# Second block's borders: the queries' projection k-tile by k-tile with the meta tokens turned later, squares of H beside its additions, lambda's exponentials behind the keys' conversions

## The reference, cut to what matters

```
h = concatenate([meta, x])                       # x: the first block's rms_norm(h, final_norm)
for l in range(2):
    hn = rmsnorm(h, norm_gain[l])
    proj = hn @ w_in[l]                          # dq dk dv dg fq fk fv ff fg
    dq, dk = partial_rope(dq), partial_rope(dk)
    lam = exp(sum(lambda_q1*lambda_k1)) - exp(sum(lambda_q2*lambda_k2)) + lam_init
    do = rmsnorm(diff_attention(dq, dk, dv, lam)) * (1 - lam_init) * silu(dg)
    fo = forgetting_attention(fq, fk, fv, cumsum(log_sigmoid(ff + bias))) * silu(fg)
    h = h + concatenate([do, fo]) @ w_out[l]
out = rmsnorm(h, final_gain)                     # the 256 rows behind the meta tokens
```

## Time and profile before

| | us |
|---|---|
| median of 3 runs | 1762.01 (1761.96 to 1763.62) |
| the profiled execution's own time | 1760.65 |
| its span | 1758.8 |
| TensorE matmul busy | 1630.2 (93%) |
| TensorE weight load busy | 1364.9 (78%) |
| VectorE busy | 1230.9 (70%) |
| ScalarE busy | 1040.4 (59%) |

### The profile page before, as it was taken

One profiled execution on the slowest core, in us unless ns is written; L12 is line 12 of the kernel. 1 busy time (PEld: TensorE's weight loads), 2 busy tenths in 40 slices (PEclk: granted clock), 3 DMA queues, 4 the chain that ended last, 5 costly groups with the idle time before them and its releaser, 6 DMA issues.

```text
span 1758.8 us, 21550 instructions
## 1 busy us (share of the span) xinstructions
PE 1630.2 (93%) x8649; PEld 1364.9 (78%) x8649; DVE 1230.9 (70%) x1295; ACT 1040.4 (59%) x1246; POOL 64.9 (4%) x64
## 2 busy tenths in 40 slices
PE   5997999988869999999999999999998988899887
PEld 5876888877758888888888888888877877778866
DVE  3655555457648888888888888888885566545665
ACT  4644444345547776777766777677675446444463
POOL 0000000011110000000000000000000300003000
PEclk9998999998969999999999999999997999889989
DMA  7422555552219989999998999999997542345410
GB/s 244 144 96 96 165 173 189 191 185 94 75 54 307 404 320 359 333 334 379 321 356 313 386 349 343 325 325 398 312 327 179 99 118 87 51 100 111 125 48 37
DMA packets 133080, 389.30 MB, mean 221 GB/s; under 512 B 8694, under 2 KB 14266, under 8 KB 132844
## 3 DMA queue, kind: packets, MB, share of 16 engines
q1 hardware_dynamic: 132692, 387.15, 65.2%
q10 hardware_dynamic: 280, 0.69, 0.1%
HBM read 386.77 MB, written 1.05 MB: 220 GB/s over the span
## 4 chain that ended last, share of the span: by engine, by line
PE 79%; DVE 9%; ACT 8%; issue 4%; DMA 0%; ACTq 0%; DVEq 0%; POOL 0%
PE psum L353 25%; PE psum L355 23%; PE psum L354 23%; ACT whi L179 4%; DVE wlo L189 4%; PE psum L412 1%; PE psum L1492 1%; PE psum L1544 1%; DVE Ss L1191 1%; PE psum L2152 1%; DVE mx L1196 0%; PE psum L1573 0%; PE psum L1574 0%; ACT hh L1603 0%; ACT sil L1598 0%
## 5 line engine op out<-in xcount | busy, mean ns | idle before, releaser
L189 DVE TENSOR_TENSOR wlo<-raw,whi 128x2048 fp32r<-128x2048 f32 (+1 forms) x286 | 629.7, 2211 | 254.3 <-ACT whi L179 253.6
L179 ACT ACTIVATE whi<-raw 128x2048 fp32r<-128x2048 f32 (+1 forms) x286 | 526.3, 1847 | 255.8 <-PE psum L355 255.8
L353 PE MATMUL psum<-whi,xh 128*128 128x512 f32 (+1 forms) x1280 | 497.3, 389 | 17.1 <-DVE xl L2466 9.0
L355 PE MATMUL psum<-whi,xl 128*128 128x512 f32 (+1 forms) x1280 | 485.8, 380 | 0.0
L354 PE MATMUL psum<-wlo,xh 128*128 128x512 f32 (+1 forms) x1280 | 484.8, 379 | 0.0
L353 PEld LDWEIGHTS psum<-whi,xh 128*128 128x128 f32 x1280 | 242.4, 189 | 73.8 <-DVE wlo L189 12.6
L355 PEld LDWEIGHTS psum<-whi,xl 128*128 128x128 f32 x1280 | 241.9, 189 | 49.5
L354 PEld LDWEIGHTS psum<-wlo,xh 128*128 128x128 f32 x1280 | 242.6, 190 | 45.9 <-issue 0.2
L189 DVE TENSOR_TENSOR wlo<-raw_more,whi 128x2048 fp32r<-128x2048 f32 (+1 forms) x94 | 204.1, 2177 | 40.3 <-ACT whi L179 39.8
L179 ACT ACTIVATE whi<-raw_more 128x2048 fp32r<-128x2048 f32 (+1 forms) x94 | 171.2, 1826 | 53.8 <-PE psum L355 53.8
L353 PE MATMUL psum<-xh,whi 128*128 128x256 f32 (+2 forms) x552 | 164.7, 298 | 15.2 <-DVE wlo L189 13.6
(11 more groups left out here) (356 smaller groups left out, 1543.9 us busy)
## 6 DMA issues: line engine op xcount, KB each, us to landing
raw<-in_moe_w_down_dram SPq DMA_DIRECT2D x58, 1024.0 KB, 7.6
raw<-in_moe_w_gate_dram SPq DMA_DIRECT2D x43, 1024.0 KB, 6.1
raw<-in_moe_w_up_dram SPq DMA_DIRECT2D x41, 1024.0 KB, 5.7
raw_more<-in_moe_w_down_dram SPq DMA_DIRECT2D x30, 1024.0 KB, 7.7
raw<-in_w_in_dram SPq DMA_DIRECT2D x28, 1024.0 KB, 8.0
raw_more<-in_moe_w_up_dram SPq DMA_DIRECT2D x23, 1024.0 KB, 5.3
raw_more<-in_moe_w_gate_dram SPq DMA_DIRECT2D x21, 1024.0 KB, 6.2
raw<-in_moe_w_up_dram SPq DMA_DIRECT2D x23, 768.0 KB, 5.7
```

The source lines that it names most:

```text
L179: act.e.activation(self.whi[:, i % self.ns, 0:kt * n], self.place[self.slots[i]][:, 0:kt * n], ACT.Copy, scale=1.0).then_inc(self.s_hi)
L189: dve.e.tensor_tensor(self.wlo[:, i % self.ns, 0:kt * n], self.place[self.slots[i]][:, 0:kt * n], self.whi[:, i % self.ns, 0:kt * n].bitca ...
L353: pe.e.matmul(o, lh, rh, start=start, stop=False)
L355: return pe.e.matmul(o, ll, rh, start=False, stop=stop)
```

## The change

- First border: ScalarE squares each half of H as soon as VectorE has added to it, into the unused half of a landing place, in place of waiting behind the meta tokens' square root; an extra square root of one column (to `st[:, 59:60]`) stands ahead of them, and the meta tokens' own root behind the squares of H. VectorE forms U before the meta tokens' reciprocal.
- Both layers: the queries' projection runs k-tile by k-tile over all four column groups (`dq(k)`), in banks 0 to 3; the turned tiles use banks 4 to 7. In layer 0 four k-tiles are turned first, then one more behind each of the first four `dq(k)`. In layer 1 the two token tiles of all eight k-tiles are turned first (two k-tiles to a bank), and the meta tokens' eight tiles between `dq(6)` and `dq(7)`; the keys wait for those.
- Layer 1: the meta rows' second square, root, reciprocal and scaling stand behind the token rows' high and low parts; three new VectorE instructions split the turned meta tiles.
- ScalarE and VectorE convert `dk`'s first piece in layer 0 right behind the last high and low parts; lambda's exponentials and differences stand behind the conversions and evictions of `dq` and `dk`.

The diff, cut to its core:

```diff
@@ mid_act
         squares(act, "meta0", 2, [(M, 16)], raw_more[:, fn_slot - RAW, D:2 * D])
-        root(act, "meta0", st[0:16, 2:3])
+        act.wait_ge(n_act.at("meta0", "sq"))
+        act.e.activation(st[0:16, 59:60], st[0:16, 2:3], ACT.Sqrt, bias=0.0, scale=1.0).then_inc(s_mid)
         for n, (t, c) in enumerate(((H, 40), (U, 48))):
             for i, (j, half) in enumerate(HALVES):
-                act.wait_ge(*([u_dve.at(j, half), (m_sq, i + 1)] if n else [h_moe.at(NE - 1, j, half), experts.ends[0]]))
+                to = vvf[:, o:o + 512] if n else raw_more[:, fn_slot - RAW, D + i % 2 * 512:D + i % 2 * 512 + 512]
+                if n:
+                    act.wait_ge(u_dve.at(j, half), experts.ends[0])
+                else:
+                    act.wait_ge(h_moe.at(NE - 1, j, half), *([(m_sq, i - 1)] if i > 1 else []))
...
+            if n == 0:
+                root(act, "meta0", st[0:16, 2:3])
@@ mid_dve
+        dve.wait_ge((s_mid, 1))
         mean(dve, "meta0", st[0:16, 2:3], D, 1e-6)
-        invert(dve, "meta0", st[0:16, 2:3])
         for j, half in HALVES:
...
+        invert(dve, "meta0", st[0:16, 2:3])
@@ pe
-            turn(pe, b, [(ox[0:16, 2, :], 16, 0), (xn[:, 0, :], 128, 16), (xn[:, 1, :], 128, 144)],
-                 scaled_at(b, s_meta.at(l)), {i: [] for i in range(8)})
-            run(standing_steps(pe, ("dq", l), G4, [0, 1, 2, 3], nq, x, [[], [], [x(6)], [x(7)]], x0=x0))
-            run(standing_steps(pe, ("dk", l), G4, [4, 5, 6, 7], NT, x, [[x(2)], [x(3)], [x(4)], [x(5)]]))
+            def dq(k):
...
+                for j in range(4):
...
+                    ins = mm3(pe, psum[:, j, 0:nq], wh[:, k % 4, c], wl[:, k % 4, c], xh[:, k, x0:x0 + nq], xl[:, k, x0:x0 + nq],
+                              k == 0, k == 7)
...
+            if l == 0:
+                for k in range(4):
+                    turned_x(k).then_inc(s_turn.end(b, k))
+                for k in range(8):
+                    dq(k)
+                    if k < 4:
+                        turned_x(k + 4, x(k)).then_inc(s_turn.end(b, k + 4))
             else:
+                for k in range(4):
+                    turned_x(k, f_w.at(0, last_unit), f_w.at(0, last_unit - 1),
+                             *([o_add.at(0, 1, 0, 0), o_add.at(0, 1, 0, 1)] if k > 1 else []))
+                    turned_x(k + 4).then_inc(s_turn.end(b, k))
+                for k in range(8):
+                    dq(k)
+                    if k == 6:
+                        pe.wait_ge(s_meta.at(1), x(4))
+                        for kk in range(8):
+                            ins = pe.e.transpose(psum[:, 4, kk * 16:(kk + 1) * 16], ox[0:16, 2, kk * 128:(kk + 1) * 128],
+                                                 ident[0:16, 0:16])
+                        ins.then_inc(m_turned.end(0))
+                pe.wait_ge(m_x.at("low"))
+            run(standing_steps(pe, ("dk", l), G4, [4, 5, 6, 7], NT, x, [[x(4)], [x(5)], [x(6)], [x(7)]]))
@@ act
             if l:
+                act.wait_ge(W.passed(P[("out", 0, 1, 1)]))
+                for k in range(4):
+                    high(k)
+                W.hi_to(act, P[("dq", l)] + 2)
+                for k in range(4, 8):
+                    high(k)
+                act.wait_ge(o_add.at(0, 1, 0, 1), o_sqH.at(0, 0, 0))
+                act.e.activation(rp2[0:16, :], M[:, 512:1024], ACT.Square, bias=0.0, scale=1.0,
+                                 accum_out=st[0:16, 47:48]).then_inc(o_sqH.end(0, 0, 1))
                 root(act, mi, mv)
...
-                act.wait_ge(lamd.at(1, 1, "sum"))
-                act.e.activation(lm[:, :, 0:2], lm[:, :, 0:2], ACT.Exp, bias=0.0, scale=1.0).then_inc(lam_exp)
             for c, name in ((0, "dq"), (4, "dk")):
...
+            if l == 0:
+                act.wait_ge(lamd.at(1, 1, "sum"))
+                act.e.activation(lm[:, :, 0:2], lm[:, :, 0:2], ACT.Exp, bias=0.0, scale=1.0).then_inc(lam_exp)
@@ dve
             if l:
+                for k in range(4):
+                    low(k)
+                W.lo_to(dve, P[("dq", l)] + 2)
+                for k in range(4, 8):
+                    low(k)
                 dve.wait_ge(o_sqH.at(0, 0, 1))
...
                 dve.e.tensor_scalar(ox[0:16, 2, :], M, mv, None, ALU.mult).then_inc(s_meta.end(l))
+                dve.wait_ge(m_turned.at(0))
+                dve.e.tensor_tensor(xh[:, :, 0:16], src, g, ALU.mult).then_inc(m_x.end("high"))
+                dve.e.tensor_tensor(w, src, g, ALU.mult).then_inc(m_x.end("product"))
+                dve.wait_ge(m_x.at("product"))
+                dve.e.tensor_tensor(xl[:, :, 0:16], w, xh[:, :, 0:16].bitcast(F32), ALU.subtract).then_inc(m_x.end("low"))
...
+                W.lo_to(dve, P[("dq", l)] + NS)
...
+            for name in ("dq", "dk"):
+                W.lo_to(dve, P[(name, l)] + 1 + NS)
+            if l == 0:
                 dve.wait_ge((lam_exp, 1))
...
-            for name in ("dq", "dk"):
-                W.lo_to(dve, P[(name, l)] + 1 + NS)
```

More of the change, by code:

```diff
@@ L323, in body @@
     TURNED = [(x, k) for x in TURNS for k in range(4 if x in ("b0 out", "b1 out") else 8)]
-    s_turn, s_xhi, s_xlo = steps("x_turned", *TURNED), steps("x_high", *TURNED), steps("x_low", *TURNED)
+    s_xhi, s_xlo = steps("x_high", *TURNED), steps("x_low", *TURNED)
+    s_turn = steps("x_turned", *[(x, k) for x, k in TURNED if x != "b1" or k < 4])
     OUTS = [("gla", 2), ("swa", 2)]
@@ L1793, in body @@
     f_a = count_on(ended_swa[13], LUf)
+    m_turned = count_on(ended_swa[14], [(0,)])
+    m_x = count_on(ended_swa[15], [("high",), ("product",), ("low",)])
     pv2 = steps("att_pv", *LU)
@@ L1946, in make_layer, with turned_in @@
         OUT = [(0, t, h) for h in range(2) for t in range(nt)] + [(1, t, h) for t in range(lt, -1, -1) for h in range(2)]
+        last_unit = len(units_of[0]) - 1
+        def turned_in(k):
+            return 4 + k % 4, k // 4 * T if l else 0
         def unit_f(t, i):
@@ L2028, in pe @@
         def pe(pe):
[L2029 to L2037 removed]
+            tiles = [(xn0[:, 0, :], 128, 16), (xn0[:, 1, :], 128, 144)] if l == 0 else [(ox[:, 0, :], 128, 0), (ox[:, 1, :], 128, 128)]
@@ new lines, in pe, with turned_x @@
+            if l == 0:
+                pe.wait_ge(*experts.ends)
+                tiles = [(ox[0:16, 2, :], 16, 0), *tiles]
+            def turned_x(k, *free):
+                pe.wait_ge(*scaled_at(b, *([] if l else [s_meta.at(0)]))[k // 4], *free)
+                bk, o = turned_in(k)
+                for src, m, off in tiles:
+                    ins = pe.e.transpose(psum[:, bk, o + off:o + off + m], src[:, k * 128:(k + 1) * 128], ident[0:m, 0:m])
+                return ins
+            def dq(k):
+                i = P[("dq", l)] + k // 4
+                wh, wl = W.views(i)
+                pe.wait_ge(W.lo(i), x(k))
+                for j in range(4):
+                    if l and k == 0:
+                        pe.wait_ge(top2.at(0, last_unit, "s") if j < 2 else t_lo.at(0, last_unit))
+                    c = slice(j * 128, (j + 1) * 128)
+                    ins = mm3(pe, psum[:, j, 0:nq], wh[:, k % 4, c], wl[:, k % 4, c], xh[:, k, x0:x0 + nq], xl[:, k, x0:x0 + nq],
+                              k == 0, k == 7)
+                    if j < 3 and k == 7:
+                        ins.then_inc(acc.end(("dq", l), j))
+                if k % 4 == 3:
+                    ins.then_inc(W.s_passed)
@@ L2169, in act, with high @@
         def act(act):
-            if l:
+            def high(k):
+                bk, o = turned_in(k)
+                act.wait_ge(s_turn.at(b, k % 4 if l else k), *([s_xlo.at(b, k - 4)] if l and k > 3 else []))
+                act.e.activation(xh[:, k, x0:NT], psum[:, bk, o:o + nq], ACT.Identity, bias=0.0,
+                                 scale=pc[:, G_N2[l] + k:G_N2[l] + k + 1]).then_inc(s_xhi.end(b, k))
+            if l:
+                act.wait_ge(W.passed(P[("out", 0, 1, 1)]))
[7 more added lines that the diff above has]
+                                 accum_out=st[0:16, 47:48]).then_inc(o_sqH.end(0, 0, 1))
                 root(act, mi, mv)
[L2172 to L2175, removed]
-            else:
-                high_by_gain(act, b, NT, G_N2[l])
+            else:
+                for k in range(8):
+                    high(k)
+                W.hi_to(act, P[("dq", l)] + NS)
                 block1_out(act)
-                act.wait_ge(lamd.at(1, 1, "sum"))
-                act.e.activation(lm[:, :, 0:2], lm[:, :, 0:2], ACT.Exp, bias=0.0, scale=1.0).then_inc(lam_exp)
             for c, name in ((0, "dq"), (4, "dk")):
@@ L2328, in act @@
             act.e.activation(st[0:16, 58:59], st[0:16, 24:25], ACT.Sqrt, bias=0.0, scale=1.0).then_inc(s_table.end(b))
-            for n in range(len(OUT) - 4, len(OUT)):
+            for n in range(len(OUT) - 4, len(OUT) if l else len(OUT) - 1):
                 squared(n)
@@ L2334, in dve, with low @@
         def dve(dve):
-            if l:
+            def low(k):
```

(17 more changed lines are left out.)

4 lines of the change are left out of this document (3 added, 1 removed).

## The result

The changed kernel takes 1750.76 us (median of 4, 1750.11 to 1751.14) against 1762.82 (median of 4) for the kernel before: ratio 0.9936, 95% interval 0.9924 to 0.9948. Timed again later beside other kernels, it took 1751.75 (median of 5) against 1759.84, ratio 0.9946 (0.9933 to 0.9959). Over its nine executions the median is 1751.1, over the 45 of before that were timed beside the experiments 1761.6: 10.4 us. The two profiled executions differ by 9.7 us (1760.65 and 1750.99). Two executions are left out of every median as slow ones: one of e (1855.36 us, granted clock 0.833) and one of before (5552.99 us).

A forecast was written before the change was run, and what follows sets the result against it. TensorE, with 79% of the chain that ended last, was taken as the bound, idle and then at half clock at two borders. 1.9 + 6.1 - 0.9 = 7.1 us off 1762.01 gives 1754.9, range 1750.5 to 1759.8.

The forecast's parts named there:

- The likeliest case: Both borders get shorter: 7.1 us faster in all, 1754.9 us; chance 0.50.
- more of it: Rival: clock rises at 1333.4 at the first border and holds through the second's wait; 9.5 us faster, 1752.5; chance 0.16.
- the half case: Rival: clock rises at 1340, falls in the second border's transposes and wait; 3.4 us faster, 1758.6; chance 0.19.
- First border, until TensorE starts: First border: VectorE's sum starts at 1325.3, 1.6 us sooner, and TensorE at 1327.3.
- First border, projection: Layer 0's queries: clock rises at 1336.6, midway between 1333.4 and 1340; keys start at 1347.6, 1.9 us sooner.
- Second border: Layer 1's start: token rows no longer wait for the meta rows, so the keys start 6.1 us sooner.
- No wait at `dq(4)`: Second border: the fifth k-tile's low part is in time by half a microsecond, so TensorE doesn't wait for it.
- The clock's fall in that wait: Second border: the wait of about 1.9 us for `wlo` can let the clock fall; 0.9 us taken off.
- Moved at no cost: Lambda's exponential, the transfers and the queries' evictions: covered at their new places, costing no time.
- The rule against it: Both borders: full clock doesn't engage for transposes, so they could cost the clock in layer 1 and hold it down in layer 0.

The follow-up runs named there:

- e: Changed kernel with layer 1's conversion of the keys' first piece ahead of the meta rows' root and VectorE's wait for the turned meta tiles: 1751.46 us, ratio 0.9937.
- b: Changed kernel with layer 0's queries in the old order, all 24 transposes first, then piece by piece: 1754.98 us, ratio 0.9962.
- a: Changed kernel with the first border's squares, U and norms in their old order: 1753.58 us, ratio 0.9949.
- d: Changed kernel with lambda's exponentials and differences back ahead of the conversions: 1750.5 us, ratio 0.9936.
- h: Kernel before, old order, with 14 unused matmuls of 512 columns in TensorE's wait at the second border: 1760.59 us, ratio 0.9994.
- c: Changed kernel with layer 1's start as before, meta rows normed first, 24 transposes, queries piece by piece: 1758.16 us, ratio 0.9979.
- i: Changed kernel with 11 unused matmuls in TensorE's wait at the first border: 1750.74 us, ratio 0.9944.
- f: Changed kernel with 24 unused matmuls of 512 columns in TensorE's wait at the first border: 1748.99 us, ratio 0.9931.
- g: Changed kernel with both the keys' first piece converted ahead of the meta wait and 24 unused matmuls at the first border: 1750.02 us, ratio 0.9930.
- j: Changed kernel with 11 unused matmuls at the first border and the keys' first piece converted ahead of the meta wait: 1750.62 us, ratio 0.9941.
- changed again: The changed kernel timed once more, with no further edit, against the kernel before: 1751.75 us, ratio 0.9946.

## Why the prediction was right

It forecast 7.1 us; 9.7 in the profiled executions, 10.4 over all, 12 in the comparison. The likeliest case was right in its mechanism, and the size came out as in the case called more of it (9.5), or above it. That 1750.76 lies inside the range is luck: it is 0.26 us above the lower end, and this end does not follow from its working. 9.5 us off 1762.01 and a microsecond more is 1751.5, not 1750.5 (and the half case with a microsecond is 1759.6, not 1759.8).

- **First border, until TensorE starts.** 1.6 forecast; from the experts' last products it was 1.87 (10.62 to 8.75), and 1.67 to 1.68 between executions with the same clock in those products. VectorE's sum was forecast at 1325.3 and started at 1325.15, released by VectorE itself.
- **First border, projection.** The term that was mis-sized. I put the clock's rise in the middle, at 1336.6; it came at 1333.8, close to the early end of 1333.4. Transposes between groups of matmuls did not hold it down: it came 3.6 us behind the first matmul here, with a k-tile's transposes between, and 3.5 in b, with none. The keys started at 1345.99, not 1347.6: 3.5 in place of 1.9. A k-tile's transposes among matmuls at full clock cost 0.5 (from 1335.80 back to the 1335.44 of the first, and the fill behind them), in the 0.4 to 0.8 given. Experiment b puts order and clock at 1.2 of it, a the earlier start at 1.0 to 1.7, each from one execution, and depending on where the clock falls and rises.
- **Second border.** Forecast from the end of TensorE's last product (1552.85, where VectorE's last addition starts) to `dq(0)` 1.8; from the same point of the changed kernel (1549.80) to 1551.44 it was 1.64. To the keys 16.1, measured 15.55; before 22.27, so the gain is 6.7 for a forecast of 6.1, 5.2 with the clock's fall. No wait at `dq(4)`. The eight small transposes took 0.6, not 1.2. The three splitting instructions took 0.29, 0.28 and 0.29, forecast 0.3. The wait of TensorE for `wlo` was forecast at 1.9 us with VectorE's standing wait as its cause; it was 1.59 with that cause, and e removed it by that step alone.
- **The clock's fall in that wait** was priced at 0.9. The clock stayed at 1.00 in every profiled execution with it: 0.9 too much taken off. Of the two stretches shown for this price, the second holds a wait of 1.43 us and not one of about 2; that three of six waits of 1.85 to 2.42 us in before's attention let the clock fall is right.
- **Moved at no cost.** Lambda, the transfers and the evictions: held (d, and 171.6 and 171.7 from the values to the end). TensorE's values ran through.
- **The rule against it** did not come true: the transposes at the start of layer 1 (1549.6 to 1551.4) stand at 1.00, and so do the 24 mixed ones of h, which the prediction had for the rule. The half of the rule that holds here is the other one: through 6.4 us of transposes with no matmul between them the clock did not rise from 0.50 (before at both borders, b, c and h's first border). And h shows that the mixed transposes are not slow by the clock alone: 4.04 against 6.37 us for 24.
- **Not forecast:** the attention stages differ by up to 3.0 us (190.7 to 193.6) and 2.0 us (171.6 to 173.6) between executions. The largest differences come with a fall of the clock behind waits of 2.3 to 2.4 us that no edit touches.

Open: why the medians over all favour the changed kernel by another 0.7 us. The mean granted clock of those 45 executions of before lies at 0.960 to 0.964, that of the changed kernel's nine at 0.964 to 0.968, so it would fit more half clock before; only a profile of those executions would show where.

## What to carry to other kernels

Where one engine sets the end, look for rows of work that wait for a small straggler (here 16 of 272), and let the rest start without it; then look at once at what is queued behind the straggler's new wait on each engine. A gain of a microsecond or two ahead of a stage with waits of about 2 us may be given back there by the clock, so compare stretches between marks, not single times. Filling a wait with unused matmuls pays only if they end when the real work is there, and their length changes with the clock that they find.

## What the runs showed of the hardware

- The 24 transposes with 16-row tiles among them take 6.37 us at half clock and 4.04 at full (0.83 and 0.53 a k-tile for three): less than a factor of two. Sixteen full tiles took 1.84 us at full clock, 0.115 each, and 3.3 at half.
- The same wait of TensorE left the clock at 1.00 in one execution and was followed by a fall in another: 2.26 us (the changed kernel; b, where it fell 1.3 us behind the wait's end at 1420.91) and 2.39 to 2.40 us (the changed kernel; e, where it fell 0.9 us behind the end at 1634.12).
- The wait of 3.02 us ahead of the experts' last products is alike in all thirteen executions. The clock fell inside it in four (c, e, h, i), 1.2 to 1.6 us behind its end in six (before, b, d, f, g, j), and in the three others (changed, changed again, a) only in the idle time after the products.
- 14 matmuls of 512 columns in a wait of 3.2 us kept the clock at full through it and through the 24 transposes behind it (h); behind 11 of them and 2.36 us idle it was at 1.00 to the end of the idle time and fell as the transposes began, to 0.50 (i).
